# Prompt attention outputs: four transpositions into a whole bank and a sum on the vector engine, in place of a product with a stacked identity

## The chip, the cores and the metric

The kernel runs on one core of a Trainium2 chip. The metric is device time in microseconds (us) of one execution. The engines are named as in the profile: PE is TensorE's matmuls, PEld its weight loads, DVE is VectorE, ACT is ScalarE, POOL is GpSimd, SP is SyncE, which issues DMAs.

## What is computed

One decoder layer for two groups of requests that share weights: a prompt of 1024 tokens and 64 sampled tokens (8 sequences of 8). The layer is an RMSNorm, one input projection, a mixer of three parts (NSA attention, gated linear attention, a short convolution), an output projection and a second RMSNorm. The part at issue is the NSA attention of the prompt. Its core in the reference, for each query head and each of the branches "selected" and "window", is

```
p_s = masked_softmax(jnp.einsum('bqhgd,bqhkd->bqhgk', qs, kv_sel[..., 0, :]), m_s)
o_s = jnp.einsum('bqhgk,bqhkd->bqhgd', p_s.astype(dt), kv_sel[..., 1, :])
...
p_w = masked_softmax(jnp.einsum('bqhgd,bkhd->bqhgk', qs, kv_band[:, :, 0]), m_w)
o_w = jnp.einsum('bqhgk,bkhd->bqhgd', p_w.astype(dt), kv_band[:, :, 1])
return gates[..., 0:1] * o_c + gates[..., 1:2] * o_s + gates[..., 2:3] * o_w
```

There are 8 query heads of 64 channels in 2 groups of 4; the prompt has 16 blocks of 64 tokens and the top 16 are taken, so the selected branch is plain causal attention over all earlier tokens, and the window branch is causal attention over the last 512. Everything is float32.

## The kernel before

`hybrid_step` runs three stages, each a block with one program per engine and a barrier behind it: `project` (most of the input projection), `attend_prompt` (prompt attention, with the rest of the projection between its steps) and `tail` (sample attention, gated linear attention, output projection). The change lies in `attend_prompt`, which covers about 290 to 730 us of the span.

`attend_prompt` works through 32 **units** of 128 queries: 2 groups of heads, in each 8 tiles of queries, for each tile first the selected branch (even unit) and then the window branch (odd unit). A unit has four heads and `tiles_of[x]` tiles of 128 keys, 1 to 8 in the selected branch and 1 to 5 in the window branch, so the last units of each group are the long ones. A list of steps, written by `schedule()`, is the order of all engines: each engine walks the list and issues what it has to do for each step, in order, so nothing overtakes anything on an engine. The steps of a unit are

- `scores`: PE multiplies keys and queries into PSUM (lines 1084, 1088);
- `least`: DVE takes the least score of each row (L1272), and `exp`: ACT takes the exponential (L1184);
- `turn`: PE transposes the probabilities of four heads into one bank (L1099), ACT copies them rounded to `pt_hi` (L1192), DVE subtracts to get the rest, `pt_lo` (L1276);
- `sum`: PE multiplies values and `pt_hi`, then `pt_lo`, into bank 6 (L1110). The stationary operand `vs` has the rounded values and their rest side by side, so rows 0 to 63 of the sum belong to the first half of the values, rows 64 to 127 to the second half. ACT copies the finished sum to `oT` (L1200), 128 rows by 4 heads of 128 queries;
- `output`: PE turns `oT` back, so that queries are rows, and adds the two halves in the same product: the moving operand `ident2` is two 64 x 64 identities on top of each other (L1121). DVE then multiplies by gate over row sum from the bank (`scaled`, L1290) and adds to `o_acc` (L1298), into `o_acc` or, in the window branch, into `pq`. The factors themselves come from L1285 and L1287 just before.

A unit's `output` stands in the list about one unit later, among the steps of the next. The steps `query` (L1056), `c_scores` (L1063), `c_turn` (L1127), `c_values` (L1131) of the compressed branch, with a few DVE steps behind each, stand between the others. `rest` steps (L1047) are pieces of the projection that fill PE's time beside the short units, mostly in the first tiles of the first group.

`output` shares bank 7 with `query`, `c_scores`, `c_turn` and `c_values`. `spare()` lets PE write the bank only when DVE has signalled `s_spr` for its last use:

```
def spare(x):

    if place[x] > 0:
        pe.wait_ge(s_spr, place[x])
    return ps[:, 7, :]
```

After `output` DVE gives this signal with L1290.

Of the kernel before, what the change touches and what calls it, by code (L numbers as in the profile page):

```python
# [9 lines left out]
ALU = mybir.AluOpType  # L10
# [6 lines left out]
AX = mybir.AxisListType.X  # L17

P = 128
# [7 lines left out]
HD = 64  # L27
NKV, NG = 2, 4
# [582 lines left out]
def attend_prompt(nc, sem, ident, pq, pk, pn, h_hi, h_lo, prob_win, s_cst, ps, L, z_dram, qk_dram, va_dram, gate_dram, w_in, w_cmp_k, w_cmp_v,  # L611
# [164 lines left out]
    with ExitStack() as ctx:  # L776
# [19 lines left out]
        oT = sb("oT", [P, NG * P])  # L796
        scaled = sb("scaled", [P, NG, HD])
# [2 lines left out]
        least = sb("least", [P, HEADS])  # L800
        rowsum = sb("rowsum", [P, HEADS])
        factor = sb("factor", [P, 2, NG])
        ident2 = sb("ident2", [P, HD])
        pen = oT[:, 0:2 * P].rearrange("p (e c) -> p e c", e=2)
        pen_r = sb("pen_r", [P, 2, P], F32R)
        ident_r = sb("ident_r", [P, P], F32R)
# [34 lines left out]
        with nc.Block() as block:  # L841
# [67 lines left out]
            def _(pool):  # L909
# [12 lines left out]
                g.wait()  # L922
                g.did(nc.gpsimd.tensor_copy(pen_r[:, :, :], pen[:, :, :]))
                g.did(nc.gpsimd.tensor_copy(ident_r[:, :], ident[:, :]))
                g.did(nc.gpsimd.tensor_tensor(ident2[:, :], ident[:, 0:HD], ident[:, HD:P], ALU.add))
                for m, x in ((c_pen, -NEG), (c_mask, 0.0)):

                    g.did(nc.gpsimd.affine_select(out=m[:, :, :], in_=m[:, :, :], compare_op=ALU.is_ge, fill=x,
# [68 lines left out]
            def _(pe):  # L997
# [6 lines left out]
                for what, x, y in steps:  # L1004
# [30 lines left out]
                    elif what == "rest":  # L1035
                        b, c = x // NCH3, x % NCH3
                        t0, tn = CH3[c]
                        bank = REST_BANKS[x % 2]
                        if y == 0:
                            if x > 1:  # L1040
                                pe.wait_ge(s_rt, x - 1)
                            if heads_before[x] > 0:
                                pe.wait_ge(s_exp, heads_before[x])
                        if c == 0 and y % 2 == 0:
                            pe.wait_ge(s_wlo, (KD // 2) * b + y // 2 + 1)
                        for n, (ww, hh) in enumerate(((w_hi, h_hi), (w_lo, h_hi), (w_hi, h_lo))):
                            mm = nc.tensor.matmul(ps[:, bank, 0:tn], ww[:, y, :], hh[:, y, t0:t0 + tn],  # L1047
                                                  start=(y == 0 and n == 0), stop=(y == KD - 1 and n == 2))
                        mm.then_inc(s_rest, 1)
                    elif what == "query":  # L1050
                        if x % NT == 0:
                            pe.wait_ge(s_klo, 6 * (x // NT) + 6)
                        pe.wait_ge(s_qst, x + 1)
                        out = spare(("q", x))
                        for g in range(NG):
                            mm = nc.tensor.transpose(out[:, g * P:(g + 1) * P],  # L1056
                                                     q_st[:, g, :, :].rearrange("p a d -> p (a d)"), ident[:, :])
                        mm.then_inc(s_sp, 1)
                    elif what == "c_scores":
                        out = spare(("cs", x))  # L1060
                        for g in range(NG):
                            for q in (q_hi, q_lo):
                                mm = nc.tensor.matmul(out[:, g * NB:(g + 1) * NB],  # L1063
                                                      q[:, x % 2, g * P:(g + 1) * P], kcT[:, :],
                                                      start=(q is q_hi), stop=(q is q_lo))
                        mm.then_inc(s_sp, 1)
                    elif what == "scores":
                        i, br = x % PER_KV // 2, x % 2
                        j0, j1 = span(x)
                        h = NG * x + y  # L1070
                        if h >= 2:
                            pe.wait_ge(s_exp, h - 1)
                        if items_before[h] > 0:
                            pe.wait_ge(s_rt, items_before[h])
                        for c in range(j0, j1 + 1, 4):
                            n = min(4, j1 + 1 - c) * P
                            bank = 2 * (y % 2) + (c - j0) // 4
                            edges = []
                            if c + n // P > j1:
                                edges.append((n - P, 0))  # L1080
                            if c == j0 and br == 1 and i >= WIN // P:
                                edges.append((0, 1))
                            for q in (q_hi, q_lo):
                                mm = nc.tensor.matmul(ps[:, bank, 0:n], q[:, i % 2, y * P:(y + 1) * P],  # L1084
                                                      kT[:, br, c * P:c * P + n],
                                                      start=(q is q_hi), stop=(q is q_lo and not edges))
                            for to, edge in edges:
                                mm = nc.tensor.matmul(ps[:, bank, to:to + P], ident_r[:, :],  # L1088
                                                      pen_r[:, edge, :], start=False,
                                                      stop=((to, edge) == edges[-1]))  # L1090
                        mm.then_inc(s_qk, 1)
                    elif what == "turn":
                        t = first_tile[x] + y
                        if y == 0:
                            pe.wait_ge(s_exp, NG * (x + 1))
                        if t >= 2:
                            pe.wait_ge(s_ptl, t - 1)
                        for g in range(NG):
                            mm = nc.tensor.transpose(ps[:, turn_bank(t), g * P:(g + 1) * P],  # L1099
                                                     prob[x % 2][:, g, y * P:(y + 1) * P], ident[:, :])  # L1100
                        mm.then_inc(s_pt, 1)
                    elif what == "sum":
                        t = first_tile[x] + y
                        if y == 0:
                            pe.wait_ge(s_vlo, 2 * (x // PER_KV) + x % 2 + 1)
                            if x > 0:
                                pe.wait_ge(s_otc, x)
                        for s, buf in ((s_pth, pt_hi), (s_ptl, pt_lo)):
                            pe.wait_ge(s, t + 1)
                            mm = nc.tensor.matmul(  # L1110
                                ps[:, 6, :],
                                vs[:, x % 2, span(x)[0] + y, :, :].rearrange("p a d -> p (a d)"),
                                buf[:, t % PTS, :], start=(y == 0 and buf is pt_hi),
                                stop=(y == tiles_of[x] - 1 and buf is pt_lo))
                        mm.then_inc(s_pv, 1)
                    elif what == "output":
                        out = spare(("z", x))
                        pe.wait_ge(s_otc, x + 1)
                        for g in range(NG):

                            mm = nc.tensor.matmul(out[:, g * HD:(g + 1) * HD], oT[:, g * P:(g + 1) * P],  # L1121
                                                  ident2[:, :], start=True, stop=True)
                        mm.then_inc(s_sp, 1)
                    elif what == "c_turn":
                        out = spare(("ct", x))
                        pe.wait_ge(s_cp, x + 1)
                        nc.tensor.transpose(out[:, 0:P], c_p[:, :, :].rearrange("p g n -> p (g n)"),  # L1127
                                            ident[:, :]).then_inc(s_sp, 1)
                    elif what == "c_values":
                        out = spare(("co", x))  # L1130
                        nc.tensor.matmul(out[:, 0:NG * HD], c_pT[:, :],  # L1131
                                         vc[:, :, :].rearrange("p g d -> p (g d)"),
                                         start=True, stop=True).then_inc(s_sp, 1)
# [69 lines left out]
            def _(dve):  # L1203
# [8 lines left out]
                for what, x, y in steps:  # L1212
# [66 lines left out]
                    elif what == "output":  # L1279
                        kv, i, br = x // PER_KV, x % PER_KV // 2, x % 2  # L1280
                        if x == 0:
# [5 lines left out]
                        v.did(nc.vector.tensor_tensor(factor[:, 0, :], factor[:, 0, :], gates, ALU.mult))  # L1287
                        v.wait()
                        dve.wait_ge(s_sp, place["z", x] + 1)
                        nc.vector.tensor_tensor(  # L1290
                            scaled[:, :, :], ps[:, 7, 0:NG * HD].rearrange("p (g e) -> p g e", g=NG),
                            factor[:, 0, :].unsqueeze(2).to_broadcast([P, NG, HD]), ALU.mult
                        ).then_inc(s_spr, 1)
                        dve.wait_ge(s_spr, place["z", x] + 1)
                        acc = o_acc[:, i % 2, :, :]
                        out = acc if br == 0 else pq[:, i, kv * NG * HD:(kv + 1) * NG * HD].rearrange(
                            "p (g d) -> p g d", g=NG)
# [1337 lines left out]
```

## Time and profile before

| what | us |
|---|---|
| median of 3 runs (lowest, highest) | 1093.35 (1092.61, 1097.33) |
| the profiled execution, its time | 1089.71 |
| its span, first to last instruction | 1088.0 |
| PE busy, share of the span | 956.3, 88% |
| DVE busy, share of the span | 607.1, 56% |
| ACT busy, share of the span | 412.2, 38% |
| mean granted TensorE clock, of full speed | 0.949 |

Busy time of PE counts matmuls that overlap; the rows of PEld, the weight loads, start one after the other and show the pace more directly. "[1.24 <-DVE least L1272]" behind a row of the timeline means that the engine stood idle for 1.24 us before the instruction and that the DVE instruction of that line released it. "issue" in that place means that the profile shows no releaser.

### The profile page before, as it was taken

Reading aid. Unit: us, or ns where it says so; the run is one execution under the profiler, and the core shown is the slowest. Engines: PE = TensorE matmul, PEld = TensorE weight load, DVE = VectorE, ACT = ScalarE, POOL = GpSimd, SP = SyncE. Lnnn points to the kernel's source line nnn. Section 1 sums busy time; section 2 is a strip of 40 time slices with the busy share of each in tenths; the row PEclk is TensorE's granted clock in tenths of the full one; section 3 lists DMA queues with packets and bytes.
Section 4 is the critical chain, followed back from the end, with each engine's and each line's share of the span. In section 5 each row is a group of like instructions: output and inputs, shape, how many; then the busy total and the mean of one; then the engine's idle time right before and its main releaser. Section 6 shows DMA issues by size and latency. Waiting matters only on the chain. (4 is left out here: it accounts for less than half of the span.)

```text
span 1088.0 us, 16638 instructions
## 1 busy us (share of the span) xinstructions
PE 956.3 (88%) x5935; PEld 813.5 (75%) x5935; DVE 607.1 (56%) x1394; ACT 412.2 (38%) x892; POOL 242.2 (22%) x197
## 2 busy tenths in 40 slices
PE   3999999999799989998998799978288998989976
PEld 2999999999689877777898687764156565765654
DVE  3532010395435677886456787864954666576640
ACT  4532111111224455665244465653432343333311
POOL 3019599998100000000002300000700000000001
PEclk9899999999899999999899899998688999999988
DMA  6226534433331110000110142014224453452310
GB/s 198 86 79 207 186 133 143 153 116 98 110 94 56 34 34 8 1 1 8 41 47 22 36 117 79 1 38 149 77 71 121 136 146 113 119 160 66 92 37 29
DMA packets 106676, 93.73 MB, mean 86 GB/s; under 512 B 21101, under 2 KB 99810, under 8 KB 104482
## 3 DMA queue, kind: packets, MB, share of 16 engines
q1 hardware_dynamic: 84946, 58.65, 18.0%
q10 hardware_dynamic: 19344, 17.25, 5.4%
q0 software_dynamic: 2304, 16.78, 4.4%
q8 instruction: 47, 0.77, 0.3%
q14 instruction: 35, 0.29, 0.1%
HBM read 78.16 MB, written 18.61 MB: 89 GB/s over the span
## 5 line engine op out<-in xcount | busy, mean ns | idle before, releaser
L588 PE MATMUL ps<-w_hi,h_hi 128*128 128x264 f32 (+5 forms) x432 | 125.1, 289 | 1.1 <-DVE h_lo L457 1.1
L588 PE MATMUL ps<-w_lo,h_hi 128*128 128x264 f32 (+5 forms) x432 | 124.0, 287 | 0.0
L588 PE MATMUL ps<-w_hi,h_lo 128*128 128x264 f32 (+5 forms) x432 | 123.9, 287 | 0.0
L1276 DVE TENSOR_TENSOR pt_lo<-ps,pt_hi 128x512 fp32r<-128x512 f32 x132 | 90.8, 688 | 50.7 <-ACT pt_hi L1192 49.9
L1192 ACT ACTIVATE pt_hi<-ps 128x512 fp32r<-128x512 f32 x132 | 78.5, 597 | 79.2 <-PE ps L1099 78.4
L465 DVE TENSOR_TENSOR w_lo<-w_raw,w_hi 128x1024 fp32r<-128x1024 f32 (+2 forms) x12 | 32.1, 2679 | 120.9 <-ACT w_hi L366 120.9
L1272 DVE TENSOR_REDUCE least<-ps 128x1 f32<-128x640 f32 (+7 forms) x128 | 89.9, 702 | 12.1 <-PE ps L1088 10.7
L313 POOL TENSOR_TENSOR chunk<-chunk 128x1024 f32<-128x1024 f32 (+2 forms) x46 | 81.9, 1780 | 3.6
L588 PEld LDWEIGHTS ps<-w_hi,h_hi 128*128 128x128 f32 (+1 forms) x432 | 80.7, 187 | 1.8 <-ACT h_hi L357 1.0
L1958 POOL TENSOR_TENSOR y_row<-y_row,x_row 128x1024 f32<-128x1024 f32 (+1 forms) x8 | 19.2, 2406 | 277.4 <-DVE y_row L2606 277.4
L588 PEld LDWEIGHTS ps<-w_lo,h_hi 128*128 128x128 f32 (+1 forms) x432 | 80.8, 187 | 0.0
L588 PEld LDWEIGHTS ps<-w_hi,h_lo 128*128 128x128 f32 (+1 forms) x432 | 80.5, 186 | 0.0
L2191 ACT ACTIVATE turned<-ps 128x512 f32<-128x512 f32 (+1 forms) x72 | 39.5, 548 | 96.2 <-PE ps L1967 80.2
L1084 PE MATMUL ps<-kT,q_hi 128*128 128x512 f32 (+3 forms) x192 | 72.9, 380 | 2.0 <-DVE stage_b L1247 1.3
L1047 PE MATMUL ps<-h_hi,wr_hi 128*128 128x362 f32 (+1 forms) x192 | 69.6, 363 | 1.9 <-DVE wr_lo L1241 1.9
L939 POOL MEMSET q_heads<- 128x512 f32 x1 | 0.6, 552 | 295.3 <-PE ps L1047 295.3
L1110 PE MATMUL ps<-pt_hi,vs 128*128 128x512 f32 x132 | 62.7, 475 | 3.8 <-issue 3.6
L2175 PE MATMUL ps<-wo_hi,m_hi 128*128 128x512 f32 (+1 forms) x128 | 60.7, 474 | 5.6 <-DVE m_lo L2602 5.6
L1047 PE MATMUL ps<-h_lo,wr_hi 128*128 128x362 f32 (+1 forms) x192 | 65.1, 339 | 0.0
L1047 PE MATMUL ps<-h_hi,wr_lo 128*128 128x362 f32 (+1 forms) x192 | 65.0, 339 | 0.0
L1084 PE MATMUL ps<-kT,q_lo 128*128 128x512 f32 (+3 forms) x192 | 64.5, 342 | 0.0
L588 PE MATMUL ps<-h_hi,w_hi 128*128 128x362 f32 (+1 forms) x192 | 63.3, 330 | 0.0
(374 smaller groups left out, 2404.6 us busy)
## 6 DMA issues: line engine op xcount, KB each, us to landing
kv_pages<-in_cache_slc_kv SPq DMA_DIRECT2D x256, 64.0 KB, 1.9
shared<-in_x_prompt SPq DMA_DIRECT2D x8, 512.0 KB, 3.6
w_raw<-in_w_in SPq DMA_DIRECT2D x8, 512.0 KB
wr_raw<-in_w_in SPq DMA_DIRECT2D x8, 512.0 KB, 4.0
kv_window<-in_cache_win_kv SPq DMA_DIRECT2D x4, 1024.0 KB, 5.6
wo_raw<-in_w_out SPq DMA_DIRECT2D x8, 512.0 KB, 8.2
out<-in_cache_win_kv SPq DMA_DIRECT2D x1, 4032.0 KB
x_row<-in_x_prompt ACTq DMA_DIRECT2D x7, 512.0 KB, 4.7
```

Of the source, the lines that this page charges most:

```text
L313: g.did(nc.gpsimd.tensor_tensor(out, a, b, ALU.add))
L465: nc.vector.tensor_tensor(half(w_lo, b), raw(b), half(w_hi, b).bitcast(F32), ALU.subtract).then_inc(s_wlo, 1)
L588: mm = nc.tensor.matmul(out, lhs, rhs, start=(k == 0 and i == 0), stop=(k == KD - 1 and i == 2))
L1047: mm = nc.tensor.matmul(ps[:, bank, 0:tn], ww[:, y, :], hh[:, y, t0:t0 + tn], start=(y == 0 and n == 0), stop=(y == KD - 1 and n == 2))
L1084: mm = nc.tensor.matmul(ps[:, bank, 0:n], q[:, i % 2, y * P:(y + 1) * P], kT[:, br, c * P:c * P + n], start=(q is q_hi), stop=(q is q_lo a ...
L1110: mm = nc.tensor.matmul(ps[:, 6, :], vs[:, x % 2, span(x)[0] + y, :, :].rearrange("p a d -> p (a d)"), buf[:, t % PTS, :], start=(y == 0 a ...
L1192: nc.scalar.activation(pt_hi[:, t % PTS, :], ps[:, turn_bank(t), :], ACT.Copy).then_inc(s_pth, 1)
L1272: nc.vector.tensor_reduce(least[:, h:h + 1], S(y, n), AX, ALU.min).then_inc(s_mx, 1)
L1276: nc.vector.tensor_tensor(pt_lo[:, t % PTS, :], ps[:, turn_bank(t), :], pt_hi[:, t % PTS, :].bitcast(F32), ALU.subtract).then_inc(s_ptl, 1)
L1958: nc.gpsimd.tensor_tensor(yt[q][0:R, :], yt[q][0:R, :], xr[q][0:R, :], ALU.add).then_inc(s_y[q], 1)
L2175: mm = nc.tensor.matmul(ps[0:R, bank + h, :], l[q][:, k, 0:R], w[:, k, h * 512:(h + 1) * 512], start=(k == 0 and j == 0), stop=(k == KD - ...
L2191: nc.scalar.activation(turned[0:rows, m % 2, 0:n], ps[0:rows, TN, 0:n], ACT.Copy).then_inc(s_tbe, 1)
```

## The change

The product with `ident2` becomes four transpositions with the identity, which put all 128 rows of `oT` for each head side by side: 4 x 128 columns, the whole of bank 7, where before 4 x 64 were written. The two halves are then added by a DVE reduction over pairs of elements 64 apart, from the bank into `scaled`. That reduction gives the signal `s_spr`. The multiplication by the factors follows as a DVE instruction of its own, from `scaled` to `scaled`. `ident2` and the POOL instruction that made it are gone. The list of steps is the same, and every other instruction stands where it stood.

```
-        ident2 = sb("ident2", [P, HD])
...
-                g.did(nc.gpsimd.tensor_tensor(ident2[:, :], ident[:, 0:HD], ident[:, HD:P], ALU.add))
...
                         out = spare(("z", x))
                         pe.wait_ge(s_otc, x + 1)
                         for g in range(NG):
-
-                            mm = nc.tensor.matmul(out[:, g * HD:(g + 1) * HD], oT[:, g * P:(g + 1) * P],
-                                                  ident2[:, :], start=True, stop=True)
+                            mm = nc.tensor.transpose(out[:, g * P:(g + 1) * P], oT[:, g * P:(g + 1) * P], ident[:, :])
                         mm.then_inc(s_sp, 1)
...
                         dve.wait_ge(s_sp, place["z", x] + 1)
-                        nc.vector.tensor_tensor(
-                            scaled[:, :, :], ps[:, 7, 0:NG * HD].rearrange("p (g e) -> p g e", g=NG),
-                            factor[:, 0, :].unsqueeze(2).to_broadcast([P, NG, HD]), ALU.mult
-                        ).then_inc(s_spr, 1)
+                        nc.vector.tensor_reduce(scaled[:, :, :], ps[:, 7, :].rearrange("p (g a d) -> p g d a", g=NG, a=2),
+                                                AX, ALU.add).then_inc(s_spr, 1)
                         dve.wait_ge(s_spr, place["z", x] + 1)
+                        v.did(nc.vector.tensor_tensor(
+                            scaled[:, :, :], scaled[:, :, :],
+                            factor[:, 0, :].unsqueeze(2).to_broadcast([P, NG, HD]), ALU.mult))
+                        v.wait()
                         acc = o_acc[:, i % 2, :, :]
```

## Rows read from the trace of the kernel before

**Rows 1.** Busy time by stretch: all units, then long units; columns as named.
```profile
core 0: us, PE busy (x) PEld busy (x) DVE busy (x) ACT busy (x) POOL busy (x), PEclk, DMA share, GB/s
355.00:730.00 375.00, 337.72 (x2141) 297.52 (x2139) 263.25 (x602) 202.64 (x456) 15.06 (x57) 0.98 0.11 31
436.00:496.00 60.00, 55.17 (x354) 46.62 (x353) 49.09 (x98) 39.19 (x79) 0.00 (x0) 1.00 0.00 1
```
**Rows 2.** Waits, 355 to 730 us: who waited, for whom, us in total, times, longest.
```profile
ACT prob_win L1184 <- DVE least L1272: 31.9, 30, 2.7
ACT prob_slc L1184 <- DVE least L1272: 30.4, 29, 2.8
PEld ps L1127 <- DVE scaled L1290: 9.3, 6, 1.9
```
**Rows 3.** Groups by shape, weight loads, 355 to 730 us: xcount | busy, mean ns | idle before.
```profile
L1121 PEld LDWEIGHTS ps<-ident,oT 128*128 128x128 f32 x256 | 33.4, 191 | 3.8 <-issue 1.1
L1099 PEld LDWEIGHTS ps<-ident,prob_slc 128*128 128x128 f32 x276 | 31.6, 144 | 7.9 <-ACT prob_slc L1184 4.6 <-DVE pt_lo L1276 0.6 <-issue 0.2
```
**Rows 4.** Timeline of weight loads: start, length, instruction; a turn, then an output.
```profile
482.21 0.59 PEld L1099 LDWEIGHTS ps<-ident,prob_win 128*128 128x128 f32 x4
482.77 0.19 PEld L1110 LDWEIGHTS ps<-pt_hi,vs 128*128 128x128 f32 x1
...
485.47 1.09 PEld L1121 LDWEIGHTS ps<-ident,oT 128*128 128x128 f32 x8
486.48 0.19 PEld L1084 LDWEIGHTS ps<-kT,q_hi 128*128 128x128 f32 x1
```
**Rows 5.** Groups by shape, DVE, 355 to 730 us.
```profile
L1290 DVE TENSOR_TENSOR scaled<-ps,factor 128x256 f32<-128x256 f32 x32 | 13.6, 425 | 6.8 <-PE ps L1121 5.9
L1272 DVE TENSOR_REDUCE least<-ps 128x1 f32<-128x512 f32 x16 | 11.0, 686 | 1.8 <-PE ps L1088 1.8
```
**Rows 6.** Groups by shape, DVE, whole span: a reduction over strided PSUM elements.
```profile
L2408 DVE TENSOR_REDUCE imp<-ps 128x32 f32<-128x256 f32 x4 | 1.7, 422 | 0.4 <-PE ps L2003 0.3
```
**Rows 7.** Timeline of all engines behind the output of unit 9, a long one.
```profile
449.73 0.42 DVE L1290 TENSOR_TENSOR scaled<-ps,factor 128x256 f32<-128x256 f32 x1
450.19 0.42 DVE L1298 TENSOR_TENSOR pq<-o_acc,scaled 128x256 f32<-128x256 f32 x1
...
451.78 0.82 DVE L1272 TENSOR_REDUCE least<-ps 128x1 f32<-128x640 f32 x1
...
452.64 0.79 ACT L1184 ACTIVATE prob_win<-ps,least 128x640 f32<-128x640 f32 x1 [1.24 <-DVE least L1272]
...
453.25 0.42 PEld L1099 LDWEIGHTS ps<-ident,prob_slc 128*128 128x128 f32 x4 [0.30 <-DVE pt_lo L1276]
```
**Rows 8.** Timeline of weight loads behind the output of unit 5: bank 7.
```profile
402.23 1.09 PEld L1121 LDWEIGHTS ps<-ident,oT 128*128 128x128 f32 x8
405.20 0.14 PEld L1127 LDWEIGHTS ps<-ident,c_p 128*128 128x128 f32 x1 [1.88 <-DVE scaled L1290]
```
**Rows 9.** Timeline of DVE: idle time in units 2, 14, 16 and 31.
```profile
379.37 0.53 DVE L1247 SCALAR_TENSOR_TENSOR stage_b<-stage_b,ps 128x362 f32<-128x362 f32 x1 [0.99 <-ACT stage_b L1165]
539.84 0.42 DVE L1290 TENSOR_TENSOR scaled<-ps,factor 128x256 f32<-128x256 f32 x1 [1.76 <-PE ps L1121]
577.99 0.43 DVE L1290 TENSOR_TENSOR scaled<-ps,factor 128x256 f32<-128x256 f32 x1 [0.92 <-PE ps L1121]
728.84 0.42 DVE L1290 TENSOR_TENSOR scaled<-ps,factor 128x256 f32<-128x256 f32 x1 [2.23 <-PE ps L1121]
```
**Rows 10.** Timeline of weight loads: outputs 8 and 9, then 24 and 25.
```profile
436.66 1.09 PEld L1121 LDWEIGHTS ps<-ident,oT 128*128 128x128 f32 x8
448.17 1.09 PEld L1121 LDWEIGHTS ps<-ident,oT 128*128 128x128 f32 x8
650.69 1.09 PEld L1121 LDWEIGHTS ps<-ident,oT 128*128 128x128 f32 x8
663.77 1.09 PEld L1121 LDWEIGHTS ps<-ident,oT 128*128 128x128 f32 x8
```
**Rows 11.** Busy time by stretch, columns as in rows 1: between outputs 24 and 25.
```profile
658.00:662.00 4.00, 3.73 (x18) 3.10 (x17) 2.39 (x7) 2.67 (x6) 0.00 (x0) 0.65 0.46 128
```

## The prediction

> **What bounds the kernel now.** I first read the busy time by stretch. Between 355 and 730 us, where all 32 outputs lie, PE is busy for 337.7 of 375 us and DVE for 263.3 [rows 1]. That looks like a stage bound by PE with room on DVE. In the long units the picture is tighter: in 60 us PE has 55.2 and DVE 49.1 [rows 1], 92% and 82%, and DVE's share leaves out the 0.04 us that each semaphore step costs it. So I read the waits next. ACT waits 62.3 us for DVE's `least` alone, in 59 waits [rows 2]. That is the loop that paces a long unit: least on DVE, exponential on ACT, turning on PE, `pt_hi` on ACT, `pt_lo` on DVE. Each engine is in order, so what is put on DVE ahead of a `least` delays that loop, even though PE is the busier engine. The timeline behind one output shows it (next part).
>
> **What PE gains.** The product with the stacked identity appears as eight weight loads for each output: 256 for 32 outputs [rows 3]. A turn, which is the same four transpositions of a float32 tile, appears as four [rows 4]. Behind a product of 512 columns, eight loads hold PE from 485.47 to 486.48, 1.01 us; four transpositions in the same place take from 482.21 to 482.77, 0.56 us [rows 4]. The gain is 0.45 us for each output, 14.4 us for 32 if all of it were on the path.
>
> **What DVE pays.** L1290 takes 425 ns [rows 5], and the next instruction starts 0.46 us after it [rows 7], so a dependent step costs 0.04 us more than it is long. The multiplication stays at 0.46 us (256 elements either way; I take no gain from reading SBUF). What is new is the reduction. It reads 512 elements of PSUM and writes 256. The nearest row is the reduction of 512 elements to one: 686 ns [rows 5]. Strided reading costs nothing in a row of the same kind: 256 elements, with the summed ones apart, to 32 results in 422 ns [rows 6]. No row has 256 results of two elements each. From below it is bounded by 0.42 us (rows 6, were only the results counted), from above by 0.95 us (were every result one more element: 256 more, at the 0.26 us by which the two reductions differ). I take 0.69, since the row at 32 results shows no surcharge. DVE's extra time for each output is then 0.69 + 0.04 = **0.73 us** (0.46 to 0.99), 23.4 us for 32. The bank signal, which now comes behind the reduction and ahead of the multiplication, comes 0.69 - 0.42 = 0.27 us later than before.
>
> **What of it lies on the path.** I went through the idle time of PE's weight loads and of DVE behind all 32 outputs, counted from 0, and sorted them.
>
> - Fifteen outputs (7 to 13, 18, 23 to 29) have no wait for bank 7 directly behind them. PE runs on and would be 0.45 us early, but then it meets DVE's loop. Rows 7 are the pattern: DVE goes without a pause from `scaled` at 449.73 to `least` at 451.78; ACT has been idle 1.24 us for this `least`; PE's next turn, at 453.25, has waited 0.30 us for `pt_lo` from DVE [rows 7]. PE's gain is waited away and DVE's 0.73 us arrives in full: 15 x 0.73 = +11.0 us.
> - In thirteen (0, 1, 3 to 6, 15 to 17, 19 to 22) the next use of bank 7 stands directly behind the output, and PE waits for `scaled`, up to 1.88 us [rows 8]. In nine DVE was late for reasons of its own, so PE's earlier end buys nothing and the bank comes 0.27 us later: +2.4. In three DVE had idled about 0.26 us for PE: 0 (of the 5.9 us that `scaled` waited for PE in seven outputs [rows 5], 4.9 are the three waits of rows 9, and four share the rest). In one it had idled 0.92 us [rows 9]: 0.27 - 0.45 = -0.2. Together +2.2. What DVE has still to do behind the signal, 0.46 us more than before, is covered by its pauses of about 1 us in these short units; if that cover is too thin, up to 13 x 0.46 = 6 us come on top.
> - Output 14 has a DVE that waits 1.76 us for PE, with filling products behind it [rows 9]: -0.45. Behind output 2 DVE pauses 0.99 us for PE's products [rows 9], so 0.73 of delay leave it 0.26 us early: -0.3.
> - Output 30 keeps some +0.3, and output 31 ends the stage, with PE and DVE in series (DVE had waited 2.23 us) [rows 9]: 0.73 - 0.45 = +0.3.
>
> The sum is 11.0 + 2.2 - 0.7 + 0.5 = **+13.0 us**. The POOL instruction lies where POOL is idle, 0. The bank is used at the same places, DMAs and SP are untouched, and the tail moves as a whole behind the barrier. The profiled execution took 1089.71 us, so the sum gives 1102.7; the median of the runs shown lies 3.6 us above that execution, so I forecast **1106 us**. With the reduction between its bounds (27 outputs carry it) this moves by about 7 us either way, 1099 to 1113.
>
> **Rivals.**
>
> *PE is the bound (faster).* If PE's 90% were what decides, the delays of DVE would vanish in its 112 us of pauses and the gain of 14.4 us would stay: 1079 us. It would take a DVE pause of 0.73 us or more, ended by PE's own lateness, between each output and PE's next wait. Rows 9 show such pauses in the short units, and rows 7 show none in the long ones. It needs PE's gain on most of the fifteen long outputs; if on half of them, the sum is near zero. Chance 0.08.
>
> *The delay is partly absorbed (no change).* The fifteen may each keep only a third of 0.73, because a pause in the same loop, which I read as ACT waiting for DVE, is really PE's. Then 15 x 0.25 + 1.7 is about 5.5 us or less: 1094 to 1099. Chance 0.17.
>
> *The clock falls more often (slower still).* PE's idle time grows by its gain and by the new waits. The granted clock in the long units was 1.00 in the first group [rows 1], but between outputs 24 and 25 it was 0.65 over 4 us [rows 11], which means a piece at the lower of the two levels, 1.2 in place of 2.4 GHz. Those outputs lie 13.08 us apart, and 8 and 9, the same unit of the other group, 11.51 us [rows 10]: one such piece costs 1.6 us. Against it: gaps of 1.88 us [rows 8] passed without a fall. With five more pieces the sum is 21 us, 1114. The Trainium skill (TensorE: Matmul & The Clock Gate, Part 4: PE-mode transpose) states a rule that speaks for this case: a transposing matmul does not count as PE activity for the clock gate as a product does, so the change takes counted activity away at 32 places. No row here separates that from plain idle time. Chance 0.2.
>
> *The transpositions do not come as four loads.* Every float32 transposition in the trace with the same call does, so I give it under 0.01; PE would gain nothing, and the time would be the same as forecast, since PE's gain is hardly used.
>
> **The numbers.** The forecast, with its bounds, has 0.55. A measurement of this kernel can tell about 0.5%, some 5.5 us, from no change. Slower by more than that: 0.55 + 0.2 and a little of the absorbed case, 0.77; the same: 0.15; faster: 0.08. The range reaches from the absorbed case to the clock case with the dearer reduction: 1096 to 1119.
>
> **What would show it.** L1121 should have half its loads and about 0.56 us for each output. The reduction should take 0.69 us. ACT's waits for `least` should grow by some 7 us or more, and PE's idle time between 355 and 730 us by about 27 (14.4 gained, 13 waited). The distance from output 8 to 9 should go from 11.5 to about 12.2 us. I am wrong if that distance is unchanged or shorter, or if the reduction takes under half a microsecond or close to one. If the long units keep their length wherever the clock is full, and only the clock column is lower, the clock rival is right and my sum is wrong.

## The result and the profile after

The changed kernel takes 1119.95 us (median of 4 runs, 1114.99 to 1122.74), the kernel before 1094.0 us on the same chip: a ratio of 1.0216, 95% interval 1.0179 to 1.0253. A second comparison of the same two kernels gave 1117.37 against 1096.11, 1.0191 (1.0165 to 1.0218). The change costs 21 to 26 us. The forecast was +13, 1106 us in a range of 1096 to 1119: the direction was right, the size about half of what was measured. Of the two medians 1117.37 lies just inside the range and 1119.95 just past it. The ratio, taken on the 1093.35 us from which the forecast was made, gives 1117.0.

The profiled execution took 1121.24 us with a span of 1119.5 and a mean granted clock of 0.927. From its page, beside the busy time and the granted clock in the 40 slices:

```profile
PE 965.4 (86%) x5807; PEld 811.6 (72%) x5807; DVE 627.8 (56%) x1426; ACT 412.7 (37%) x892; POOL 242.5 (22%) x196
...
PEclk9999999999789999998899799996777999999988
```

Shares hardly moved. The span grew by 31.5 us: 27.3 between the first and the last `scaled` (370.9 us before, 398.1 after), 1.2 ahead of them and 3.1 behind. The part ahead and behind scatters between executions; the second profiled execution of the changed kernel has a span of 1112.3 us, of which 394.2 in the stage. So the stage is where to look. Its busy time, columns as in [rows 1], which it answers to:

```profile
355.00:758.00 403.00, 342.71 (x2023) 293.88 (x2021) 285.95 (x637) 203.47 (x459) 15.21 (x57) 0.94 0.10 29
```

The waits in it, answering to [rows 2]:

```profile
ACT prob_win L1180 <- DVE least L1268: 47.9, 34, 2.9
ACT prob_slc L1180 <- DVE least L1268: 39.0, 29, 3.2
PEld ps L1123 <- DVE scaled L1286: 14.5, 6, 3.2
```

ACT waits 86.9 us for DVE's `least`, 24.6 more than before. The weight loads' wait for bank 7 rose from 9.3 to 14.5 us, again in six waits. And the pieces themselves, by shape (xcount | busy, mean ns | idle before), answering to [rows 3, 5]:

```profile
L1286 DVE TENSOR_REDUCE scaled<-ps 128x256 f32<-128x512 f32 x32 | 22.1, 692 | 4.5 <-PE ps L1118 3.5
L1118 PEld LDWEIGHTS ps<-ident,oT 128*128 128x128 f32 x128 | 15.8, 140 | 5.3 <-issue 1.1
L1289 DVE TENSOR_TENSOR scaled<-scaled,factor 128x256 f32<-128x256 f32 x32 | 13.6, 425 | 1.1
```

Half the loads, as forecast; the reduction takes 692 ns where 0.69 us was taken; the multiplication stays at 425 ns. What stands behind the output of unit 9, the place of [rows 7]:

```profile
458.87 0.69 DVE L1286 TENSOR_REDUCE scaled<-ps 128x256 f32<-128x512 f32 x1
459.60 0.43 DVE L1289 TENSOR_TENSOR scaled<-scaled,factor 128x256 f32<-128x256 f32 x1
460.06 0.43 DVE L1296 TENSOR_TENSOR pq<-o_acc,scaled 128x256 f32<-128x256 f32 x1
...
461.65 0.83 DVE L1268 TENSOR_REDUCE least<-ps 128x1 f32<-128x640 f32 x1
...
462.51 0.80 ACT L1180 ACTIVATE prob_win<-ps,least 128x640 f32<-128x640 f32 x1 [2.44 <-DVE least L1268]
...
463.12 0.42 PEld L1097 LDWEIGHTS ps<-ident,prob_slc 128*128 128x128 f32 x4 [0.85 <-DVE pt_lo L1272]
```

From the start of `scaled` to that of `least` it was 2.05 us and is 2.78, +0.73. ACT's wait grew from 1.24 to 2.44 us, PE's wait for `pt_lo` from 0.30 to 0.85. PE came earlier and stood longer.

### The profile page after: what moved, and what is told of

It reads as the page before. It is cut to its first block and busy times, and to the rows that moved or that the text cites. A ratio compares the mean times of both kernels' runs of the same rounds, so it can differ in the third digit from the quotient of the medians.

```text
span 1119.5 us, 16413 instructions
## 1 busy us (share of the span) xinstructions
PE 965.4 (86%) x5807; PEld 811.6 (72%) x5807; DVE 627.8 (56%) x1426; ACT 412.7 (37%) x892; POOL 242.5 (22%) x196
## 5 line engine op out<-in xcount | busy, mean ns | idle before, releaser
L1082 PE MATMUL ps<-kT,q_hi 128*128 128x512 f32 (+3 forms) x192 | 75.4, 393 | 4.4 <-ACT prob_slc L1180 3.1
L1045 PE MATMUL ps<-h_hi,wr_hi 128*128 128x362 f32 (+1 forms) x192 | 72.0, 375 | 1.9 <-DVE wr_lo L1237 1.9
L1108 PE MATMUL ps<-pt_hi,vs 128*128 128x512 f32 x132 | 65.4, 495 | 5.1 <-issue 4.7
L1180 ACT ACTIVATE prob_slc<-ps,least 128x128 f32<-128x128 f32 (+7 forms) x64 | 47.5, 741 | 48.1 <-DVE least L1268 47.8
```

The source lines that it names most:

```text
L1108: mm = nc.tensor.matmul(ps[:, 6, :], vs[:, x % 2, span(x)[0] + y, :, :].rearrange("p a d -> p (a d)"), buf[:, t % PTS, :], start=(y == 0 a ...
L1180: nc.scalar.activation(prob[x % 2][:, y, 0:n], S(y, n), ACT.Exp, scale=-1.0, bias=least[:, h:h + 1], accum_out=rowsum[:, h:h + 1]).then_in ...
```

## The experiments

Twelve experiments ran. One of them is the changed kernel again and one a repetition. Ratios are to the kernel before on the same chip, with 95% intervals. **Distance** below is the time from the start of one unit's `scaled` to that of the next, from DVE's timeline of a profiled execution; "distance 9" is from output 9 to 10, and "unit 9" below means that stretch.

### Which part costs

**One DVE step more in the kernel before**, `before_extra_step`: PE's part stays.

```
                         dve.wait_ge(s_spr, place["z", x] + 1)
...
+                        v.did(nc.vector.tensor_tensor(scaled[:, :, :], scaled[:, :, :], scaled[:, :, :], ALU.max))
+                        v.wait()
```

> The kernel before with one more DVE step of 128 x 256 elements (0.46 us, the maximum of scaled with itself) between the bank signal and the addition. Theory 1: +0.46 us in the fifteen long outputs, 7 us, little in the others, and some more pieces at the lower clock at 1.3 us each: 1100 to 1110 us. Theory 2: the clock as before, 17 us at the lower level: 1101. If DVE had slack: 1094.

Measured: 1109.91 us, 1.0126 (1.0073 to 1.0179). One step of 0.43 us, behind the bank signal, on an engine that is busy 56% of the span, costs 14 us. That this is near 32 x 0.46 is chance: the distances below show the step in full in the long units and not at all in most short ones, and some 4 of the 14 us are put down to the clock further below.

**PE's part alone**, `turn_light`: four transpositions, and the old single multiplication, which reads the first half of each head. It leaves out the sum of the two halves.

```
-                        nc.vector.tensor_reduce(scaled[:, :, :], ps[:, 7, :].rearrange("p (g a d) -> p g d a", g=NG, a=2),
-                                                AX, ALU.add).then_inc(s_spr, 1)
+                        nc.vector.tensor_tensor(
+                            scaled[:, :, :], ps[:, 7, :].rearrange("p (g e) -> p g e", g=NG)[:, :, 0:HD],
+                            factor[:, 0, :].unsqueeze(2).to_broadcast([P, NG, HD]), ALU.mult
+                        ).then_inc(s_spr, 1)
...
-                        v.did(nc.vector.tensor_tensor(
-                            scaled[:, :, :], scaled[:, :, :],
-                            factor[:, 0, :].unsqueeze(2).to_broadcast([P, NG, HD]), ALU.mult))
-                        v.wait()
```

> The four transpositions of the change with DVE's work of before: one multiplication that reads only the first half of each head's 128 rows (the second half of the values, their rounding rest, is left out of the sum). Theory 1: PE's gain is mostly waited away, DVE's loop is as before: 1085 to 1095 us, 17 to 30 us at the lower clock. Theory 2: the lower clock grows as in the change (over 40 us) and the time is 1100 or more. A rival that calls PE the bound: 1080.

Measured: 1093.87 us, 0.9984 (0.9964 to 1.0003). PE has 128 loads less and the time is nearly the same, 2 us less with an interval that reaches no change: PE's gain is worth next to nothing by itself. The distances show where the little lies: behind outputs 15, 18, 29 and 30 they are 0.40, 0.13, 0.24 and 0.64 us shorter than before, 1.4 us together.

**The same DVE work behind the dearer product**, `product_wide` and `product_wide_again`:

```
-                            mm = nc.tensor.transpose(out[:, g * P:(g + 1) * P], oT[:, g * P:(g + 1) * P], ident[:, :])
+                            mm = nc.tensor.matmul(out[:, g * P:(g + 1) * P], oT[:, g * P:(g + 1) * P], ident[:, :],
+                                                  start=True, stop=True)
```

> The changed kernel, but the turning back is a product with the 128 x 128 identity again (eight weight loads an output, about 1.0 us) into the whole bank; DVE does the reduction and the multiplication as in the change. Theory 1 (DVE's 0.73 us sits in the loop of the long units, and PE's longer pauses make the clock fall): PE's 0.45 us an output was waited away anyway, so the time stays near the change's, 1112 to 1121 us, with 8 to 13 pieces at the lower clock in the prompt stage (the change has 15 pieces' worth, 53 us; before has 17 us). Theory 2 (the clock falls because transpositions take the place of products): the clock recovers to about 17 us at the lower level, and the time falls to about 1107, the 13 us that DVE alone costs.

> The changed kernel beside product_wide_again on one chip. Theory 1 (only PE's idle time lowers the clock, and the transpositions add 0.45 us of it an output): the mean granted clock is a little lower than with products (0.929 against 0.935 in the first runs) and the time 2 to 4 us longer. If the first runs only differed by chip: the same clock and time as product_wide_again.

> As the first run of it: 1116 to 1118 us, clock 0.935. If the transpositions alone cost clock, after_again is 3 us longer beside it; if they don't, the two agree.

Measured: 1116.79, 1.0192 (1.0154 to 1.023); in the second group, side by side, the change 1117.37, 1.0191 (1.0165 to 1.0218), and this kernel 1117.89, 1.0187 (1.0158 to 1.0215). By shape, L1118 is back at the form of before, and the stage keeps the length that the change gave it (columns as in [rows 1]):

```profile
L1118 PEld LDWEIGHTS ps<-ident,oT 128*128 128x128 f32 x256 | 33.4, 191 | 3.8 <-issue 1.1
...
358.30:754.20 395.90, 347.71 (x2125) 302.59 (x2125) 281.33 (x623) 201.08 (x450) 15.21 (x57) 0.95 0.10 30
```

The loss needs no transposition: the DVE work alone brings it. This also bears on the rule that was weighed in the clock rival (the Trainium skill, TensorE: Matmul & The Clock Gate, Part 4: PE-mode transpose). If transpositions made the clock fall and products didn't, this kernel should be clearly faster than the change, and it is as fast; the 2 to 4 us that were expected between the two side by side did not show. Its mean clock is a little higher, 0.935 against 0.931 over nine runs each; whether transpositions or merely PE's shorter work make that difference, no run here separates.

### The law of the long units

These distances hold at full granted clock in every column but the starred ones, in which one piece at the lower clock lies:

| distance | before | change | extra step | turn light |
|---|---|---|---|---|
| 7 | 10.53 | 11.27 | 11.00 | 10.54 |
| 9 | 12.30 | 13.05 | 12.77 | 12.31 |
| 11 | 13.35 | 14.08 | 13.83 | 13.37 |
| 12 | 10.18 | 12.51* | 10.64 | 10.19 |
| 25 | 12.30 | 13.04 | 12.77 | 12.30 |
| 27 | 13.38 | 14.08 | 13.84 | 13.36 |
| 28 | 10.18 | 12.50* | 10.66 | 10.17 |

The change adds 0.70 to 0.75 us to a long unit, the one extra step 0.46 to 0.49, PE's gain alone 0.02 at most either way. What DVE is given arrives in full. One long unit is an exception: distance 29, at full clock in all four, goes from 10.94 to 11.43, 0.49 us, since there PE's gain counts too. In the short units 0, 6, 16, 17 and 22 the change adds 0.25 to 0.30, the later bank signal; the extra step, which comes behind the signal, adds 0.03 or less there.

**The change in one kind of unit only**, `change_long_only` (outputs 7 to 13, 18, 23 to 29) and `change_short_only` (the other seventeen): the change behind `if x in CHANGED`, the code of before in the `else`.

```
+    LONG = (*range(7, 14), 18, *range(23, 30))
+    CHANGED = LONG
```

> The change for the fifteen outputs that the prediction called long (7 to 13, 18, 23 to 29) alone; the other seventeen as before. The prediction's sort: +11.0 us at full clock, each of them 0.73 us longer, and most of what the lower clock adds: 1108 to 1114 us beside 1096. If the seventeen short ones carry a good part of the change's 21 to 26 us, it is 1105 or less.

> The change for the other seventeen outputs alone. The prediction's sort: +2.0 us, so 1097 to 1100 us. If the delay behind the bank signal is not covered in the short units, or their clock falls: 1102 to 1108.

Measured: 1111.64, 1.015 (1.0126 to 1.0174), and 1100.85, 1.0058 (1.0038 to 1.0078). That is +16.7 and +5.9 us, together 22.6, the whole change. The prediction's sort had +11.0 and +2.0.

### The clock

The starred distances show what lies on top. Unit 12 in the two profiled executions of the same changed kernel, first one and then the other (columns as in [rows 1]; the third figure from the end is the granted clock):

```profile
499.88:512.39 12.51, 10.51 (x58) 8.75 (x57) 9.16 (x14) 8.04 (x17) 0.00 (x0) 0.86 0.00 0
```

```profile
500.61:511.52 10.91, 8.89 (x58) 7.43 (x57) 9.07 (x14) 7.74 (x17) 0.00 (x0) 1.00 0.00 0
```

PE's instructions are the same; at 0.86 the unit takes 1.60 us longer, and at 1.00 it is the old 10.18 plus 0.73. The fall doesn't follow from the unit's own pauses: in both executions the longest pause of the loads in it is 1.84 or 1.85 us. Nor does it need changed code. In `change_long_only` everything up to output 6 is as before, and yet distance 5 went from 13.24 to 14.82 us; first before, then `change_long_only`:

```profile
404.73:417.97 13.24, 11.03 (x68) 9.66 (x68) 8.08 (x15) 6.23 (x14) 0.00 (x0) 1.00 0.05 15
```

```profile
406.25:421.07 14.82, 12.60 (x68) 11.07 (x68) 8.09 (x16) 6.23 (x14) 0.00 (x0) 0.88 0.04 14
```

Distance 5 holds such a piece in twelve of the fourteen profiled executions, with and without the change; before and `after_fill` are the two without it.

Distance 3 is another kind. It is 11.55 to 11.82 us at 0.85 or 0.86 in all six executions in which DVE does more behind outputs 2 and 3 and PE is not filled up: the change twice, `product_wide` twice, `change_short_only` and `before_extra_step`. It is at full clock in the other eight. This piece comes with the added DVE work.

So some pieces go with the added work and others come and go between executions, and their number has to be compared over many runs. There are 51 runs of the kernel before, on three chips, each with its mean granted clock. They lie between 1088.64 us at 0.949 and 1100.41 us at 0.938 (the lowest clock, 0.935, has 1098.82 and 1100.28), and a straight line through them falls by 0.70 us for each 0.001 of clock, give or take 0.07 (mean 0.941 and 1095.3 us). Taken at that price, each kernel's difference from this mean splits:

| kernel (runs) | mean clock | mean us more | of it clock | at equal clock |
|---|---|---|---|---|
| change, both comparisons (9) | 0.931 | 22.8 | 7.2 | 15.6 |
| `product_wide`, both (9) | 0.935 | 21.8 | 4.0 | 17.8 |
| `change_long_only` (6) | 0.934 | 16.3 | 4.7 | 11.6 |
| `change_short_only` (6) | 0.938 | 5.2 | 2.5 | 2.7 |
| `before_extra_step` (4) | 0.935 | 14.6 | 4.2 | 10.4 |
| `turn_light` (10) | 0.940 | -1.5 | 0.6 | -2.1 |

The last column is an estimate, since it takes the line of one kernel for all of them. It fits in itself: `product_wide` without PE's gain costs 2.2 us more than the change, and `turn_light`, PE's gain alone, 2.1 less than before. It says that the change costs some 15 us by its added DVE work and some 7 by the clock (8.4 in the first comparison, 6.3 in the second), and that the long and the short units, each at equal clock, cost 11.6 and 2.7 us. With one extra step on DVE the clock falls too, without any change on PE.

**PE kept busier**, `after_fill`: the four products and then the four transpositions, into the same bank.

```
                         for g in range(NG):
+                            mm = nc.tensor.matmul(out[:, g * P:(g + 1) * P], oT[:, g * P:(g + 1) * P], ident[:, :],
+                                                  start=True, stop=True)
+                        for g in range(NG):
                             mm = nc.tensor.transpose(out[:, g * P:(g + 1) * P], oT[:, g * P:(g + 1) * P], ident[:, :])
```

> The changed kernel with the four products in front of the four transpositions, into the same bank, so twelve weight loads an output (about 1.45 us) and PE's pauses shorter by 0.9 us. Theory 1: the time at the lower clock falls well below the change's 53 us, but PE's longer step is on the path behind the outputs where DVE waits for PE: 1108 to 1122. Theory 2 (transpositions do not count): the products add counted work too, so it gives the same; if instead neither matters the time is the change's plus 0.9 us for each output, up to 1140.

Measured: 1117.53, 1.0179 (1.0136 to 1.0223), the same as the change. Its stage and unit 3, then a wait that in the change was 3.5 us in 3 outputs:

```profile
357.90:752.00 394.10, 351.22 (x2249) 307.24 (x2249) 280.83 (x622) 201.48 (x451) 15.25 (x57) 0.98 0.10 30
384.13:394.36 10.23, 9.39 (x60) 8.54 (x60) 8.12 (x17) 5.72 (x15) 0.00 (x0) 1.00 0.01 2
...
DVE scaled L1289 <- PE ps L1121: 13.3, 22, 2.7
```

The clock of the stage is back at 0.98, and unit 3, 11.82 us in the change at 0.86, takes 10.23, the 9.96 of before and 0.27. But DVE now waits 13.3 us for PE in 22 outputs, and the clock's gain is spent on it. This is not a test of the clock alone: filling takes its own time. An experiment that changes the clock and nothing else was not tried, so the clock's share stays the estimate of the table.

### Is there anything on the other side?

If DVE's loop were the one bound, work taken off it should come back as fully as added work costs. Four kernels move work from DVE to POOL, which is busy for only 15 of 375 us of the stage before. POOL signals each add to a semaphore, and DVE waits for it before it writes `scaled` again.

```
+                    nc.gpsimd.tensor_tensor(out, acc, scaled[:, :, :], ALU.add).then_inc(s_w2z, 1)
...
+                        if x > 0:
+                            dve.wait_ge(s_w2z, x + 2)
...
-                        v.did(nc.vector.tensor_tensor(out, acc, scaled[:, :, :], ALU.add))
-                        v.wait()
```

`before_add_pool` does this in the kernel before:

> The kernel before with the addition into o_acc or pq on POOL instead of DVE, which takes 0.46 us off DVE's loop for each output. Theory 1, read the other way round from before_extra_step: the long outputs come 0.46 us closer together, 15 x 0.46 = 7 us, and fewer pieces at the lower clock: 1080 to 1090 us beside 1095. If DVE's load only hurts above that of before: 1095. POOL's addition should take about 0.8 us and hide.

Measured: 1092.7, 0.9965 (0.9941 to 0.9988), less than expected. Of the 0.46 us taken off DVE, the long units at full clock give back 0.06 (distances 11 and 27) to 0.41 (distance 26). Two reasons can be told apart. In distances 7, 9, 23 and 25 it is 0.19, and there a DVE copy into `c_p` takes 0.47 in place of 0.18 us because POOL is at work (last section): 0.19 and that 0.29 make up the step. In distances 11 and 27 the copy keeps its 0.18 us, so something other than DVE holds them. In the short units POOL's slower add costs as well: DVE waits 5.6 us for it, in four places, before it writes `o_acc`.

`after_mult_add_pool` moves the multiplication and the add of the changed kernel:

> The changed kernel with the multiplication and the addition on POOL; DVE keeps the factors and the reduction, 0.73 us in place of the 0.92 us that the multiplication and addition took before, and the bank comes 0.27 us later than before. Theory 1: long outputs 0.19 us closer together than before, nine outputs 0.27 us further: about 1090 to 1096 us, some 25 us under the change. If the clock falls because of transpositions, 1100 or more.

Measured: 1094.62, 0.9986 (0.9966 to 1.0006): the loss of the change is gone, and nothing more. The short distances 0, 6, 16, 17 and 22 are still 0.13 to 0.15 us longer than before.

`turn_light_add_pool` has both reliefs, four transpositions (first half only) and the add on POOL:

> turn_light (four transpositions, DVE's multiplication of the first half alone, the second half of the sum left out) with the addition on POOL: PE has 0.45 us and DVE 0.46 us less an output than before. If two chains, PE's and DVE's, are nearly tied in the long units, so that either gain alone is lost (turn_light 0.998, before_add_pool 0.9965), both together count: the long outputs come 0.4 to 0.5 us closer, 6 to 7 us, and the time is 1084 to 1090 us. If something else bounds them, 1092 as before_add_pool.

Measured: 1085.85, 0.9911 (0.9884 to 0.9937). PE's gain alone gave 2.0 us, DVE's relief alone 3.4 us, and together they give 9.1. Distance 11 shows it: 13.37 with the one, 13.29 with the other, 12.96 with both. So in such units two chains lie nearly level, one through DVE and one through PE. More DVE work counts in full, since no other chain covers it; less counts only until PE's chain is met. Distances 7 and 9 are 10.3 and 12.1 us with both, as with the add on POOL alone: where the blocked copy keeps DVE long, PE's gain still buys nothing.

`after_most_pool` is the changed kernel with gate product, multiplication and add on POOL; DVE keeps the reciprocal and the reduction.

> The changed kernel with gate product, multiplication and addition on POOL; DVE keeps the reciprocal and the reduction, 0.93 us an output where before had 1.32 and the change has 2.05; PE has 0.45 us less than before. Two nearly tied chains: 1086 to 1092 us beside 1096, the fastest that computes everything. If POOL's SBUF traffic slows DVE's copies, or the 0.27 us later bank signal weighs more: 1094 to 1097.

Measured: 1089.64, 0.9952 (0.9936 to 0.9969), with the whole computation: faster than both kernels. DVE's part of an output is here well under that of before (0.93 us against 1.32), and some of PE's gain is collected; in `after_mult_add_pool`, where it was only 0.19 us under, the time came level and no better. Its rows by shape:

```profile
L1316 DVE TENSOR_REDUCE scaled<-ps 128x256 f32<-128x512 f32 x32 | 21.3, 666 | 3.4 <-PE ps L1150 3.4
L946 POOL TENSOR_TENSOR scaled<-scaled,factor 128x256 f32<-128x256 f32 x32 | 19.7, 615 | 17.7 <-DVE scaled L1316 17.6
L955 POOL TENSOR_TENSOR o_acc<-o_acc,scaled 128x256 f32<-128x256 f32 x16 | 11.8, 736 | 1.3
...
L1346 DVE TENSOR_TENSOR o_acc<-ps,factor 128x256 f32<-128x256 f32 x14 | 5.9, 420 | 11.5 <-POOL pq L955 8.6 <-PE ps L1159 2.9
```

The last row shows what POOL costs in return: the next write of `o_acc` by DVE now waits 8.6 us in all for POOL's add.

## Why the prediction was right and wrong

**Right: what bounds.** A DVE busy 56% of the span was taken as the path, because the long units' loop runs through it without a pause. Six of the long distances at full clock in both profiled executions confirm it (7, 9, 11, 23, 25 and 27: 0.70 to 0.75 us for a forecast 0.73). The seventh, 29, grew by 0.49 only. Distance 8, the one named in the prediction, is 13.32 us with a low-clock piece inside: 11.47 + 0.73 leaves 1.1 for that piece.

**Right: the price list.** Reduction 0.692 us (0.69 taken between 0.42 and 0.95), multiplication 0.425, PE's gain next to nothing (`turn_light`), bank 7 later by 0.27: the distances 0, 6, 16, 17 and 22, all short units, grew by 0.25 to 0.30. PE is not the bound (first rival), and nothing was absorbed in the long units (second rival).

**Right: the two sums, at equal clock.** Long units +11.0 forecast and 11.6 found; all others +2.0 and 2.7; the whole 13.0, and 14.3 by these two or 15.6 by the change itself. These are estimates that can be off by a us or two, as the intervals of the two ratios show.

**Wrong: the clock was left out of the sum.** This is the step that failed. The third rival was weighed as something that would happen in place of the forecast, with a chance of 0.2; it came on top of it, for some 7 us of the 21 to 26. Its price per piece was right or somewhat high: 1.6 us from [rows 10, 11], 1.60 in unit 12, 1.1 in distance 8. The number of pieces was what failed. The profiled execution of before was among those with the highest clock, 0.949 where 51 runs have 0.941 on average, so its rows showed full clock almost throughout, and gaps of 1.88 us that passed without a fall were taken for safe ones. In the profiled execution of the change, seven distances that had been at full clock (3, 5, 8, 10, 12, 26, 28) hold a piece, and 13, 19 and 20 one more than before. These seven grew by 14.0 us in all; the added DVE time explains 5 x 0.73 + 2 x 0.27 = 4.2 of it. Two of the seven are not the change's doing. Distance 5 holds its piece in `turn_light` and in `change_long_only` too, and distance 8 in `change_short_only`, where outputs 7 to 9 are as before (13.07 us at 0.87); there the profile of before was the lucky one.

That luck alone is not the miss. By the line through the 51 runs 0.949 in place of 0.941 is worth 5.6 us, and the forecast had already added 3.6 us to come from that execution to the median. What it lacked is the fall from 0.941 to 0.931 that the change brings. That the result still lies at the range's end is partly luck too: the end was reached with the dearer reduction on top of the clock case, and the reduction was not dearer.

Two of them are short units. The thin cover that the sum named for these (up to 6 us) is not what made them dear: at full clock the short distances 0, 1, 4, 6, 16, 17 and 22 grew by 0.25 to 0.38. Unit 3 shows how the change lengthens a pause of PE. Its loads wait for bank 7 (changed kernel, idle before in brackets):

```profile
385.68 0.14 PEld L1123 LDWEIGHTS ps<-ident,c_p 128*128 128x128 f32 x1 [3.18 <-DVE scaled L1286]
```

In the kernel before this wait was 1.58 us. Both parts of the change lengthen it: with PE's part alone (`turn_light`) it is 2.57 us, with DVE's part alone (`product_wide`) 2.58. Unit 3 then takes 11.82 us at 0.86. Yet the length of this pause does not decide by itself: 2.57 us in `turn_light` passed at full clock (9.95 us), and 2.05 us in `before_extra_step` did not (11.55 us at 0.85). What does decide is not shown by these runs.

**Wrong: output 2.** It was given -0.3, because DVE pauses 0.99 us there [rows 9], and grew by 0.74. The prediction took the pause for one that waits for PE's products, while the row names ACT's `stage_b`. After the change:

```profile
380.34 0.58 ACT L1180 ACTIVATE prob_win<-ps,least 128x384 f32<-128x384 f32 x1 [1.51 <-DVE least L1268]
...
381.39 0.47 ACT L1161 ACTIVATE stage_b<-ps 128x362 f32<-128x362 f32 x1
...
381.89 0.53 DVE L1243 SCALAR_TENSOR_TENSOR stage_b<-stage_b,ps 128x362 f32<-128x362 f32 x1 [0.99 <-ACT stage_b L1161]
```

The pause is still 0.99 us. Its releaser `stage_b` stands on ACT behind the exponential that waited for DVE's `least`, and it starts 3.29 us after the start of `scaled` where it was 2.56 before, +0.73. So the whole chain moved, pause and all. A pause covers a delay only where its releaser doesn't hang on the delayed engine.

**The forecast of idle time.** PE's loads were to be idle 27 us more. By busy time of the loads it is (403.0 - 293.9) - (375.0 - 297.5) = 31.6; the clock's part is in it.

## What to carry to other kernels

Read an engine's worth from the waits that end last in a unit, not from its busy share: here 0.46 us more for each output on an engine busy 56% cost 14 us, while a relief of the engine busy 88% gave 2 us until the other was relieved too. Before a pause is counted as cover, follow its releaser back and see whether it hangs on the work that is delayed. Where a change lengthens PE's pauses and the trace shows low-clock pieces already, their price belongs in the sum and not only in a rival, and one profiled execution, which may be a lucky one, does not tell their number.

## What was not expected of the hardware

A reduction of pairs 64 elements apart in PSUM, 512 elements to 256 results, takes 692 ns; the reduction of 512 elements to one takes 688 ns in the same kernel, and `pt_lo`, a subtraction of 512 elements, 688. The number of results and the stride cost nothing here. The Trainium skill (VectorE: DVE Perf Modes, Rules for kernel authors) calls `tensor_reduce` the slowest DVE op; these rows, all float32 and read from PSUM, don't show it slower than a subtraction of as many elements.

One DVE copy from SBUF to SBUF is held up by a POOL instruction that is already running, until that one ends. It is the copy into `c_p`; its rows are shown before the change (by shape over the stage) and in one place of `before_add_pool`:

```profile
L1310 DVE COPY c_p<-c_s 128x64 f32<-128x64 f32 x13 | 2.4, 184 | 0.0
```

```profile
430.25 0.77 POOL L949 TENSOR_TENSOR pq<-o_acc,scaled 128x256 f32<-128x256 f32 x1 [9.03 <-DVE scaled L1316]
...
430.60 0.47 DVE L1331 COPY c_p<-c_s 128x64 f32<-128x64 f32 x1
```

It is not a general slowing. In the four kernels with work on POOL this copy takes either 183 to 191 ns, or 350 to 1106 ns, and in each of the long cases it ends 46 to 56 ns after a POOL instruction does. DVE's multiplication that reads PSUM kept its 425 ns in `before_add_pool`. POOL needs 736 ns for the add that DVE does in 425.
